# Turning two of the four recurrent-input turns of a hybrid decoder trunk to stationary tokens, with a trip through the scratch in DRAM

## The chip, the cores and the metric

One core of one Trainium2 chip runs the whole kernel. The metric is the device time of one execution in microseconds (us), as the median of repeated runs. The engines are TensorE (PE; its weight loads are PEld), VectorE (DVE), ScalarE (ACT), GpSimd (POOL) and SyncE (SP), whose queue issues nearly all of the DMAs here (SPq in the rows).

## The reference

Two decoder layers on an input of 256 tokens by 2048 channels, all in float32. Layer 0 mixes tokens with a gated recurrent block, layer 1 with causal attention; each is followed by a squared-ReLU MLP of width 8192, and each of the four sub-layers ends in a LayerNorm of `alpha * x + sublayer(x)`. What the change touches is the beginning of layer 0:

```python
gate, u = jnp.split(x @ w_in, 2, axis=-1)          # w_in: 2048 x 4096
u = causal depthwise conv of width 4 over u, + conv_b
r = sigmoid(blockwise u @ gate_a_w + gate_a_b)      # 8 blocks of 256 channels
i = sigmoid(blockwise u @ gate_x_w + gate_x_b)
a = exp(-8 * r * softplus(-lam));  b = u * i * sqrt(1 - a*a)
h = associative scan of h_t = a_t * h_{t-1} + b_t
return (gelu(gate) * h) @ w_out
```

## The kernel before

Every matmul of the large layers is made of three products of rounded parts: each operand is split into a high part and a low remainder (`fp32r`), and high by high, low by high and high by low are added up in PSUM. A weight block is 256 rows (two chunks of 128) by 512 columns. SyncE loads it into one of 4 staging slots (`wst`, `load_block`, L272), ScalarE copies it rounded into one of 8 slots of high parts (`wh`, `split_hi`, L781), VectorE subtracts to get the low part (`wl`, `split_lo`, L1083), and TensorE uses both. The load of block b waits until block b-4 has been split by VectorE (`wl_done`). Eight blocks make a turn: 512 output columns, accumulated over all 2048 rows. The order on every engine is written out by hand: `splits(b, lo, hi)` on ScalarE and on VectorE says which blocks are split between the other pieces of work. `AHEAD` is 7: in turn t these two engines split block 7 and later of the count that starts with the turn's first block, so they work up to 7 blocks ahead of TensorE. `LATE` is 14.

The blocks are numbered through the program. The recurrent input u takes turns 0 to 3 (blocks 0 to 31), the two gate matrices take blocks 32 to 39, the gate branch takes four turns from block 40.

There are two ways to run a turn on TensorE:

- `turn` (L483, L486) keeps a 128 x 128 piece of the weights stationary and moves tokens: for each of 16 chunks and 4 column groups one matmul of 512 columns (high and low tokens side by side, against the high weights) and one of 256 columns (high tokens, low weights). The result has channels on the partitions, and its two halves are in different columns of four banks; ScalarE copies one half out (`take_hl`, L790) and VectorE adds the other (`add_hh`, L1093), which frees the banks (`psum_free`).
- `token_turn` (L495) keeps 128 tokens stationary and moves 512 weight columns: for each chunk six matmuls of 512 columns. The result has tokens on the partitions, in two banks.

Before, all four turns of u use `turn`. The gate branch (blocks 40 to 71) uses `token_turn`; its result must be turned over, since what follows works along the tokens in each channel. ScalarE copies the two banks into a buffer in an order that suits the move (`g_out`, L901) and so frees them; SyncE stores it as four DMAs of 128 KB to a scratch in DRAM (`store_g`, L315) and, once they have landed, loads it back as one DMA of 512 KB with the 32 x 32 squares in place (`read_g`, L321); VectorE transposes within the squares (`turn_g`, L1235, a STREAM_TRANSPOSE). The MLP does the same with its squares (L361, L365, L1453). Both SyncE's waits, for the banks and for the stores, stand in the same queue as the weight loads.

After each turn t of u, the group of four chunks it made goes through the convolution: ScalarE multiplies by the last tap and adds the bias (`conv_start`, L825, four activations), VectorE adds the three other taps (`conv_step`, L1162, four instructions each), ScalarE rounds (`conv_hi_part`, L818), VectorE takes the remainder (`conv_lo`, L1170). Only then can TensorE run the gates of this group. The gates (L588 to L590) are eight pieces `gb`, two for each group, each with 24 matmuls of 256 columns into a pair of banks: gb 0 uses banks 0 and 1, gb 1 banks 2 and 3, gb 2 banks 4 and 5, gb 3 banks 6 and 7, and then again from the start. What TensorE waits for there, ahead of each piece:

```python
            for gb in range(BLOCKS):
                if gb in (0, 2):
                    pe.wait_ge(psum_free, T_G + gb // 2 - 1)
                elif gb >= 4:
                    pe.wait_ge(sig_done, gb - 3)
                pe.wait_ge(pair_ready, R_CONV + 2 * (gb // 2) + 2)
                pe.wait_ge(wl_done, B_GATES + gb + 1)
```

So gb 2 needs the banks of the last turn of u (`psum_free` at 4), and the pieces from gb 4 need the sigmoids of the piece four earlier (`sig_done`, L851, on ScalarE). The softplus of `lambda` is a row of small VectorE instructions (`softplus_start`, L1136 to L1140, `softplus_series`, L1144 to L1150) between the splits.

## Time and profile before

| | |
|---|---|
| Median of 3 runs | 2082.54 us (2081.93 to 2082.73) |
| The profiled execution's own time | 2081.55 us |
| Its span, from the first to the last instruction | 2079.8 us |
| TensorE busy | 2073.0 us, 9438 matmuls |
| VectorE busy | 1267.6 us |
| ScalarE busy | 969.2 us |
| Mean DMA traffic | 217 GB/s |
| Granted TensorE clock in the 40 slices | digit 9 (90% or more of full speed) in each |

The profile is one execution; its own time lies 1.75 us above its span and 0.99 us below the median of the runs. In a timeline row stand the start, the duration, the engine, the line, the operation, output<-inputs, how many instructions are merged, and in brackets the idle time before them with what ended it. Matmuls are pipelined: the row of one is longer than the step from its start to the next start, and it is the step that counts.

### The profile page before, as it was taken

The page shows a single profiled execution, that of the slowest core. Times are in us where ns is not written, and L with a number is a line of the kernel's source. Part 1 is how long each engine was busy: PE and PEld are TensorE (multiplying, and loading weights), DVE is VectorE, ACT ScalarE, POOL GpSimd, SP SyncE. Part 2 cuts the span into 40 slices and gives each one's busy share as a digit, 9 for nine tenths or more (in the row PEclk, how much of TensorE's full clock was granted, in tenths as well). Part 3 has the DMA queues.
Part 4 walks back from the last instruction along what each step waited for, and adds up shares of the span by engine and source line. Part 5 has one row for each costly group of instructions (what it writes and reads, how often), then busy time and mean ns, then how long its engine had stood idle before and what let it go on. Part 6 is the DMA issues. An engine that isn't in the chain of part 4 may idle for free.

```text
span 2079.8 us, 27469 instructions
## 1 busy us (share of the span) xinstructions
PE 2073.0 (100%) x9438; PEld 1724.6 (83%) x9438; DVE 1267.6 (61%) x1247; ACT 969.2 (47%) x1168; POOL 21.3 (1%) x16
## 2 busy tenths in 40 slices
PE   9999999999999999999999999999999999999999
PEld 8888888888888888888888888888888888888887
DVE  6869666665555565555765565775755555555565
ACT  5595555434444443443654444454444434444442
POOL 0000010000000000000100000010000000000000
PEclk9999999999999999999999999999999999999999
DMA  8667758766766766675566667667767766766763
GB/s 259 195 207 243 257 189 264 246 199 206 237 220 185 241 225 200 214 249 173 186 209 206 210 221 233 194 212 243 229 207 221 241 200 201 240 218 224 240 214 120
DMA packets 245884, 451.34 MB, mean 217 GB/s; under 512 B 18720, under 2 KB 49696, under 8 KB 244768
## 3 DMA queue, kind: packets, MB, share of 16 engines
q1 hardware_dynamic: 239888, 440.93, 66.8%
q10 hardware_dynamic: 5904, 9.18, 1.4%
q8 instruction: 58, 0.95, 0.2%
q14 instruction: 34, 0.28, 0.0%
HBM read 421.72 MB, written 20.97 MB: 213 GB/s over the span
## 4 chain that ended last, share of the span: by engine, by line
PE 99%; DMA 0%; DVE 0%; ACT 0%; SPq 0%; issue 0%
PE ps L495 92%; PE ps L486 3%; PE ps L483 1%; PE ps L620 1%; PE ps L589 0%; PE ps L590 0%; PE ps L588 0%; PE ps L658 0%; PE ps L667 0%; DMA f<-in_x_dram 0%; PE ps L668 0%; PE ps L657 0%; PE ps L545 0%; PE ps L681 0%; PE ps L682 0%; DVE f L1335 0%
## 5 line engine op out<-in xcount | busy, mean ns | idle before, releaser
L1083 DVE TENSOR_TENSOR wl<-wst,wh 128x1024 fp32r<-128x1024 f32 x742 | 886.5, 1219 | 380.0 <-ACT wh L781 377.9
L781 ACT ACTIVATE wh<-wst 128x1024 fp32r<-128x1024 f32 x742 | 770.5, 1059 | 690.5 <-PE ps L495 400.6
L495 PE MATMUL ps<-wh,xin 128*128 128x512 f32 x3072 | 824.5, 390 | 0.0
L495 PE MATMUL ps<-wh,hid 128*128 128x512 f32 x2560 | 695.9, 390 | 0.0
L495 PEld LDWEIGHTS ps<-wh,xin 128*128 128x128 f32 x3072 | 575.7, 188 | 118.9
L495 PEld LDWEIGHTS ps<-wh,hid 128*128 128x128 f32 x2560 | 479.5, 188 | 98.9
L495 PE MATMUL ps<-wl,xin 128*128 128x512 f32 x1536 | 472.9, 389 | 0.0
L495 PE MATMUL ps<-wl,hid 128*128 128x512 f32 x1280 | 404.6, 389 | 0.0
L495 PEld LDWEIGHTS ps<-wl,xin 128*128 128x128 f32 x1536 | 288.3, 188 | 60.0
L495 PEld LDWEIGHTS ps<-wl,hid 128*128 128x128 f32 x1280 | 240.2, 188 | 50.0
L1453 DVE STREAM_TRANSPOSE f<-f 128x1024 f32<-128x1024 f32 x32 | 39.9, 1245 | 178.7 <-DMA f<-sq_by_quad 178.7
L975 ACT ACTIVATE hid<-f 128x1024 fp32r<-128x1024 f32 x32 | 34.0, 1063 | 206.5 <-DVE f L1453 206.5
L1280 DVE TENSOR_TENSOR f<-f,ps 128x1024 f32<-128x1024 f32 x36 | 43.9, 1220 | 86.9 <-PE ps L495 86.9
L486 PE MATMUL ps<-xin,wh 128*128 128x512 f32 x256 | 88.8, 397 | 0.0
L1477 DVE TENSOR_TENSOR f<-f 128x1024 f32<-128x1024 f32 x32 | 39.2, 1225 | 74.5 <-ACT f L990 74.3
L990 ACT ACTIVATE f<-ps 128x512 f32<-128x512 f32 x64 | 34.7, 595 | 79.0 <-PE ps L495 79.0
L483 PE MATMUL ps<-xin,wl 128*128 128x256 f32 x256 | 68.5, 278 | 0.0
L486 PEld LDWEIGHTS ps<-xin,wh 128*128 128x128 f32 x256 | 46.9, 188 | 9.5
L483 PEld LDWEIGHTS ps<-xin,wl 128*128 128x128 f32 x256 | 48.1, 188 | 1.4
L1459 DVE TENSOR_TENSOR hid<-f,hid 128x1024 fp32r<-128x1024 f32 x32 | 39.2, 1225 | 3.0
L912 ACT ACTIVATE f<-ps,prm 128x128 f32<-128x128 f32 x96 | 36.2, 480 | 4.1 <-PE ps L620 4.1
L454 POOL TENSOR_SCALAR f<-f,mv,tok 128x512 f32<-128x512 f32 x6 | 19.5, 3259 | 1345.7 <-DVE tok L1310 1345.7
(123 smaller groups left out, 563.8 us busy)
## 6 DMA issues: line engine op xcount, KB each, us to landing
wst<-in_mlp_w_dram SPq DMA_DIRECT2D x512, 512.0 KB, 4.7
wst<-in_moba_w_qkv_dram SPq DMA_DIRECT2D x96, 512.0 KB, 4.6
wst<-in_rg_w_in_dram SPq DMA_DIRECT2D x62, 512.0 KB, 4.5
wst<-in_rg_w_out_dram SPq DMA_DIRECT2D x32, 512.0 KB, 5.6
sq_by_quad<-f SPq DMA_DIRECT2D x128, 128.0 KB, 2.6
f<-sq_by_quad SPq DMA_DIRECT2D x32, 512.0 KB, 4.9
wst<-in_moba_w_out_dram SPq DMA_DIRECT2D x32, 512.0 KB, 5.1
f<-in_x_dram SPq DMA_DIRECT2D x8, 256.0 KB, 6.8
```

Source lines behind the costliest of these rows:

```text
L483: mm = pe.matmul(dst[:, n, 0:T], wl[:, s, w], src[:, c, 0, :], start=False, stop=(c == NC - 1))
L486: pe.matmul(dst[:, n, :], wh[:, s, w], src[:, c, :, :], start=(c == 0), stop=False)
L495: return pe.matmul(dst, src[:, c, part, a * P:(a + 1) * P], (wl if low else wh)[:, s, w], start=(c == 0 and part + low == 0), stop=(c == N ...
L781: act.activation(wh[:, off % SPLITS, :], wst[:, slot, :], ACT.Copy).then_inc(wh_done, 1)
L912: ins = act.activation(norm_t[:, c, h * P:(h + 1) * P], ps[:, bank, q * P:(q + 1) * P], ACT.Identity, scale=prm[:, gain:gain + 1], bias=pr ...
L975: act.activation(hid[:, t * GROUP:(t + 1) * GROUP, 0, :], sq_t, ACT.Copy).then_inc(sq_hi, 1)
L990: act.activation(by_part, by_col, ACT.Relu).then_inc(sq_relu, 1)
L1083: dve.tensor_tensor(wl[:, off % SPLITS, :], wst[:, off % STAGE, :], wh[:, off % SPLITS, :], ALU.subtract).then_inc(wl_done, 1)
L1280: dve.tensor_tensor(res[:, :, cols], res[:, :, cols], banks(half)[:, 0:HALVES, :], ALU.add)\
L1453: dve.transpose(sq_t.rearrange("p c (a i t) -> p i (c a) t", a=HALVES, t=32), quad.rearrange("p i (b r) -> p i b r", r=32)).then_inc(sq_tu ...
L1459: dve.tensor_tensor(hid[:, rows, 1, :], sq_t, hid[:, rows, 0, :], ALU.subtract)\
L1477: dve.tensor_tensor(sqr, sqr, sqr, ALU.mult).then_inc(psum_free, 1)
```

## The change

Turn 1 and turn 2 of u (blocks 8 to 15 and 16 to 23) now run as `token_turn`, in banks 4 and 5 and in banks 0 and 1; turn 0 and turn 3 stay as they are. What the gate branch has for its results, u now shares: the buffers and semaphores are renamed from `g_` to `in_`, the trips are counted through (trips 0 and 1 are u's, 2 to 5 the gate branch's), and ScalarE's copy (`take_in`) frees the banks. `take_hl` and `add_hh` of turns 1 and 2 are gone. VectorE turns the group over (`turn_u`), and `conv_start` of groups 1 and 2 waits for that. The convolution steps of these groups stand later in VectorE's order, and the one of group 2 now stands partly ahead of `add_hh` of turn 3. The order of the loads, the number of weight blocks and the gates' code are unchanged.

```diff
...
+        def turn_of(n):
+            return T_U + 1 + n if n < U_TOKEN else T_G + n - U_TOKEN
...
-            with sp.Fori(1, NG) as t:
-                load_turn(w_in, D + t * COLS, B_U + t * BLOCKS)
-            for gb in range(BLOCKS):
+            def store_in(n):
+                sp.wait_ge(psum_free, turn_of(n) + 1)
+                for i in range(GROUP):
+                    sp.dma_start(to_quad[i], in_out[i * 32:(i + 1) * 32, :, :]).then_inc(in_stored, 16)
+            def read_in(n):
+                sp.wait_ge(in_stored, (n + 1) * (16 * GROUP))
+                if n:
+                    sp.wait_ge(in_turned, n)
+                sp.dma_start(in_quad, by_quad.rearrange("p (i n) -> p i n", i=GROUP)).then_inc(in_back, 16)
+            def move_in(n):
+                return {2: lambda: store_in(n), 3: lambda: read_in(n)}
...
+            def load_gates(gb, b):
                 w, n0 = (rg_gate_a_w, rg_gate_x_w)[gb % 2], gb // 2 * 2
-                sp.wait_ge(wl_done, B_GATES + gb - (STAGE - 1))
+                sp.wait_ge(wl_done, b - (STAGE - 1))
...
+            with sp.Fori(1, NG - 1) as t:
+                load_turn(w_in, D + t * COLS, B_U + t * BLOCKS)
+            load_turn(w_in, D + (NG - 1) * COLS, B_U + (NG - 1) * BLOCKS, move_in(0))
+            also = move_in(1)
+            for gb in range(BLOCKS):
+                if gb in also:
+                    also[gb]()
+                load_gates(gb, B_GATES + gb)
...
-            turn(xin, 1, B_U + BLOCKS, R_X)
-            pair(xin, B_U + 2 * BLOCKS, R_X, T_U + 2)
+            token_turn(xin, 4, B_U + BLOCKS, R_X)
+            pe.wait_ge(psum_free, T_U + 1)
+            token_turn(xin, 0, B_U + 2 * BLOCKS, R_X)
+            pe.wait_ge(psum_free, T_U + 2)
+            turn(xin, 1, B_U + 3 * BLOCKS, R_X)
...
-                act.wait_ge(psum_free, T_U + g + 1)
+                if 1 <= g <= U_TOKEN:
+                    act.wait_ge(in_turned, g)
+                else:
+                    act.wait_ge(psum_free, T_U + g + 1)
...
-            for t in range(NG):
-                b = B_U + t * BLOCKS
-                if t:
-                    splits(b, t, AHEAD, AHEAD + 1)
-                    conv_start(t - 1)
-                    splits(b, t, AHEAD + 1, AHEAD + CONV)
-                    if t == 1:
-                        act.wait_ge(sp_abs, 1)
-                        act.activation(small[:, 1, :], small[:, 0, :], ACT.Exp, scale=-1.0).then_inc(sp_exp, 1)
-                    conv_hi_part(t - 1)
-                splits(b, t, AHEAD + CONV if t else BLOCKS, LATE)
-                take_hl(t % 2, b, u3[:, t * GROUP:(t + 1) * GROUP, :], hl_copied)
-                splits(b, t, LATE)
-            conv_start(NG - 1)
+            def take_in(n, first, b):
+                act.wait_ge(mm_done, b + BLOCKS)
+                if n:
+                    act.wait_ge(in_turned, n)
+                for a in range(HALVES):
+                    by_part = in_out.rearrange("p q (c a r) -> p a c q r", c=GROUP, a=HALVES)[:, a]
+                    by_col = ps[:, first + a, :].rearrange("p (c q r) -> p c q r", c=GROUP, q=GROUP)
+                    taken = act.activation(by_part, by_col, ACT.Copy)
+                taken.then_inc(psum_free, 1)
+            b, no = B_U, 0
+            splits(b, no, BLOCKS, LATE)
+            take_hl(0, b, u3[:, 0:GROUP, :], hl_copied)
+            splits(b, no, LATE)
+            b, no = B_U + BLOCKS, 1
+            splits(b, no, AHEAD, AHEAD + 1)
+            conv_start(0)
+            splits(b, no, AHEAD + 1, AHEAD + CONV)
+            act.wait_ge(sp_abs, 1)
+            act.activation(small[:, 1, :], small[:, 0, :], ACT.Exp, scale=-1.0).then_inc(sp_exp, 1)
+            conv_hi_part(0)
+            splits(b, no, AHEAD + CONV, LATE)
+            take_in(0, 4, b)
+            splits(b, no, LATE)
+            b, no = B_U + 2 * BLOCKS, 2
+            splits(b, no, AHEAD, AHEAD + 6)
+            conv_start(1)
+            splits(b, no, AHEAD + 6, LATE)
+            take_in(1, 0, b)
+            splits(b, no, LATE)
+            b, no = B_U + 3 * BLOCKS, 3
+            splits(b, no, AHEAD, AHEAD + 1)
+            conv_hi_part(1)
+            splits(b, no, AHEAD + 1, AHEAD + 6)
+            conv_start(2)
+            splits(b, no, AHEAD + 6, LATE)
+            take_hl(1, b, u3[:, 3 * GROUP:NC, :], hl_copied)
+            splits(b, no, LATE)
+            conv_hi_part(2)
+            conv_start(3)
...
-            for t in range(NG):
-                b = B_U + t * BLOCKS
-                if t:
-                    splits(b, AHEAD, AHEAD + 1)
-                    for k in range(1, CONV):
-                        splits(b, AHEAD + k, AHEAD + k + 1)
-                        conv_step(t - 1, k)
-                    splits(b, AHEAD + CONV, AHEAD + CONV + 1)
-                    conv_lo(t - 1)
-                    splits(b, AHEAD + CONV + 1, LATE)
-                else:
-                    softplus_abs()
-                    splits(b, BLOCKS, LATE)
-                (lambda: None, softplus_start, softplus_series, lambda: None)[t]()
-                add_hh(t % 2, u3[:, t * GROUP:(t + 1) * GROUP, :], hl_copied, t + 1).then_inc(psum_free, 1)
-                splits(b, LATE)
-            g = NG - 1
-            for k in range(1, CONV):
-                conv_step(g, k)
-            splits(B_GATES, AHEAD, AHEAD + 1)
-            conv_lo(g)
-            splits(B_GATES, AHEAD + 1)
-
-
+            def turn_in(n, dst):
+                dve.wait_ge(in_back, 16 * (n + 1))
+                dve.transpose(dst.rearrange("p c (a i t) -> p i (c a) t", a=HALVES, t=32),
+                              in_quad.rearrange("p i (b r) -> p i b r", r=32)).then_inc(in_turned, 1)
+            def turn_u(g):
+                turn_in(g - 1, u3[:, g * GROUP:(g + 1) * GROUP, :])
...
+            b = B_U
+            softplus_abs()
+            splits(b, BLOCKS, LATE)
+            add_hh(0, u3[:, 0:GROUP, :], hl_copied, 1).then_inc(psum_free, 1)
+            splits(b, LATE)
+            b = B_U + BLOCKS
+            splits(b, AHEAD, AHEAD + 1)
+            for k in range(1, CONV):
+                splits(b, AHEAD + k, AHEAD + k + 1)
+                conv_step(0, k)
+            splits(b, AHEAD + CONV, AHEAD + CONV + 1)
+            conv_lo(0)
+            softplus_start()
+            splits(b, AHEAD + CONV + 1)
+            b = B_U + 2 * BLOCKS
+            splits(b, AHEAD, AHEAD + 2)
+            softplus_series()
+            splits(b, AHEAD + 2, AHEAD + 5)
+            turn_u(1)
+            splits(b, AHEAD + 5, AHEAD + 6)
+            conv_step(1, 1)
+            splits(b, AHEAD + 6, LATE)
+            conv_step(1, 2)
+            splits(b, LATE)
+            conv_step(1, 3)
+            b = B_U + 3 * BLOCKS
+            splits(b, AHEAD, AHEAD + 1)
+            conv_lo(1)
+            splits(b, AHEAD + 1, AHEAD + 5)
+            turn_u(2)
+            splits(b, AHEAD + 5, AHEAD + 6)
+            conv_step(2, 1)
+            splits(b, AHEAD + 6, LATE)
+            conv_step(2, 2)
+            conv_step(2, 3)
+            add_hh(1, u3[:, 3 * GROUP:NC, :], hl_copied, 2).then_inc(psum_free, 1)
+            splits(b, LATE)
+            conv_lo(2)
+            for k in range(1, CONV):
+                conv_step(3, k)
+            splits(B_GATES, AHEAD, AHEAD + 1)
+            conv_lo(3)
+            splits(B_GATES, AHEAD + 1)
```

The first place is SyncE's queue, from the end of the loads of u to the loads of the gate matrices. Before, behind the loop that loads the last turn of u (blocks 24 to 31):

```order
L272 DMA wst<-in_rg_w_in_dram 128x2x512
L304 REGISTER_ALU
L304 COMPARE_AND_BRANCH
L309 DMA wst<-in_rg_gate_a_w_dram 128x4x256 [waits wl_done]
L309 DMA wst<-in_rg_gate_x_w_dram 128x4x256 [waits wl_done]
L309 DMA wst<-in_rg_gate_a_w_dram 128x4x256 [waits wl_done]
```

In the changed kernel (`L277` loads u's blocks 24 and on, `L326` the gate matrices, `L312` stores, `L318` loads back):

```order
L277 DMA wst<-in_rg_w_in_dram 128x2x512 [waits wl_done] x2
L312 DMA sq_by_quad<-spare 32x4x256 [waits psum_free]
L312 DMA sq_by_quad<-spare 32x4x256 x3
L277 DMA wst<-in_rg_w_in_dram 128x2x512 [waits wl_done]
L318 DMA spare<-sq_by_quad 128x1024 [waits in_stored]
L277 DMA wst<-in_rg_w_in_dram 128x2x512 [waits wl_done] x5
L326 DMA wst<-in_rg_gate_a_w_dram 128x4x256 [waits wl_done]
L326 DMA wst<-in_rg_gate_x_w_dram 128x4x256 [waits wl_done]
L312 DMA sq_by_quad<-spare 32x4x256 [waits psum_free]
L312 DMA sq_by_quad<-spare 32x4x256 x3
L326 DMA wst<-in_rg_gate_a_w_dram 128x4x256 [waits wl_done]
L318 DMA spare<-sq_by_quad 128x1024 [waits in_turned,in_stored]
```

Two trips are new: the first stands between the loads of blocks 25 and 27, with block 26 between its parts, the second between those of blocks 33 and 35, with block 34 between. Each load back waits for its stores, and the loads behind it wait with it.

The second place is VectorE while turn 3 of u runs and after it. Before (`L1083` splits a block, `L1093` is `add_hh`, which frees the banks of turn 3):

```order
L1162 SCALAR_TENSOR_TENSOR gate<-f1,prm,gate 128x253 [waits conv_link]
L1162 SCALAR_TENSOR_TENSOR gate<-f1,prm,gate 128x253 x3
L1083 TENSOR_TENSOR wl<-wst,wh 128x1024 [waits mm_done,wh_done]
L1170 TENSOR_TENSOR hid<-gate,hid 128x4x256 [waits conv_hi]
L1083 TENSOR_TENSOR wl<-wst,wh 128x1024 [waits mm_done,wh_done] x2
L1093 TENSOR_TENSOR f1<-f1,ps 128x1024 [waits hl_copied]
L1083 TENSOR_TENSOR wl<-wst,wh 128x1024 [waits mm_done,wh_done]
L1162 SCALAR_TENSOR_TENSOR gate<-f1,prm,gate 128x255 [waits conv_begun]
```

In the changed kernel (`L1117` splits, `L1209` is the transpose of group 2, `L1196` its convolution steps, `L1127` is `add_hh`):

```order
L1117 TENSOR_TENSOR wl<-wst,wh 128x1024 [waits mm_done,wh_done] x4
L1209 STREAM_TRANSPOSE f1<-spare 128x4x8x32 [waits in_back]
L1117 TENSOR_TENSOR wl<-wst,wh 128x1024 [waits mm_done,wh_done]
L1196 SCALAR_TENSOR_TENSOR gate<-f1,prm,gate 128x255 [waits conv_begun]
L1196 SCALAR_TENSOR_TENSOR gate<-f1,prm,gate 128x255 x3
L1117 TENSOR_TENSOR wl<-wst,wh 128x1024 [waits mm_done,wh_done]
L1196 SCALAR_TENSOR_TENSOR gate<-f1,prm,gate 128x254 [waits conv_link]
L1196 SCALAR_TENSOR_TENSOR gate<-f1,prm,gate 128x254 x3
L1196 SCALAR_TENSOR_TENSOR gate<-f1,prm,gate 128x253 [waits conv_link]
L1196 SCALAR_TENSOR_TENSOR gate<-f1,prm,gate 128x253 x3
L1127 TENSOR_TENSOR f1<-f1,ps 128x1024 [waits hl_copied]
L1117 TENSOR_TENSOR wl<-wst,wh 128x1024 [waits mm_done,wh_done]
```

Before, the convolution of group 2 was over when `add_hh` of turn 3 came, with three splits and `conv_lo` between them. Now the transpose and all three of group 2's steps stand ahead of it.

## Rows read from the trace of the kernel before

**Rows 1.** The page: busy time of the engines

```profile
PE 2073.0 (100%) x9438; PEld 1724.6 (83%) x9438; DVE 1267.6 (61%) x1247; ACT 969.2 (47%) x1168; POOL 21.3 (1%) x16
```

**Rows 2.** The chain that ended last: shares, then start, length, what

```profile
PE 99%; DMA 0%; DVE 0%; ACT 0%; SPq 0%; issue 0%
...
122.52 168.67 PE ps L495 x744
```

**Rows 3.** Timeline of TensorE: turn 3, gb 0, gb 2

```profile
77.12 0.63 PE L486 MATMUL ps<-xin,wh 128*128 128x512 f32 x2
...
99.32 0.28 PE L588 MATMUL ps<-hid,wh 128*128 128x256 f32 x1
...
105.07 0.28 PE L588 MATMUL ps<-hid,wh 128*128 128x256 f32 x1
```

**Rows 4.** Timeline of VectorE after block 19

```profile
57.37 1.22 DVE L1170 TENSOR_TENSOR hid<-gate,hid 128x1024 fp32r<-128x1024 f32 x1
...
60.77 0.17 DVE L1136 TENSOR_SCALAR small<-small 128x16 f32<-128x16 f32 x1
...
61.89 1.22 DVE L1093 TENSOR_TENSOR f<-f,ps 128x1024 f32<-128x1024 f32 x1
```

**Rows 5.** Timeline of ScalarE: copy of turn 1, conv_start(3), sigmoids gb 0 to 2

```profile
58.00 1.00 ACT L790 ACTIVATE f<-ps 128x1024 f32<-128x1024 f32 x1
...
103.85 2.08 ACT L825 ACTIVATE gate<-f,prm 128x256 f32<-128x256 f32 x4 [2.08 <-DVE f L1093]
...
108.19 1.57 ACT L851 ACTIVATE f<-ps,prm 128x256 f32<-128x256 f32 x4
...
110.58 1.59 ACT L851 ACTIVATE f<-ps,prm 128x256 f32<-128x256 f32 x4
...
113.91 1.62 ACT L851 ACTIVATE f<-ps,prm 128x256 f32<-128x256 f32 x4
```

**Rows 6.** Timeline of VectorE: add_hh of turn 3, twelve steps of conv 3

```profile
102.60 1.21 DVE L1093 TENSOR_TENSOR f<-f,ps 128x1024 f32<-128x1024 f32 x1
...
105.96 5.06 DVE L1162 SCALAR_TENSOR_TENSOR gate<-f,prm,gate 128x255 f32<-128x255 f32 x12 [1.01 <-ACT gate L825]
```

**Rows 7.** The page: low parts and high parts of the weight blocks

```profile
L1083 DVE TENSOR_TENSOR wl<-wst,wh 128x1024 fp32r<-128x1024 f32 x742 | 886.5, 1219 | 380.0 <-ACT wh L781 377.9
L781 ACT ACTIVATE wh<-wst 128x1024 fp32r<-128x1024 f32 x742 | 770.5, 1059 | 690.5 <-PE ps L495 400.6
```

**Rows 8.** Line L272 (loads of u), 60 to 100 us: time to landing

```profile
DMA to landing us min/median/max: 3.5/4.2/4.7
```

**Rows 9.** Timeline of SyncE: first trip of the gate branch

```profile
147.31 2.63 SPq L315 DMA_DIRECT2D sq_by_quad<-spare  x4
149.98 0.45 SPq L272 DMA_DIRECT2D wst<-in_rg_w_in_dram  x1
153.26 0.34 SPq L321 DMA_DIRECT2D spare<-sq_by_quad  x1
153.65 1.56 SPq L272 DMA_DIRECT2D wst<-in_rg_w_in_dram  x3
```

**Rows 10.** DMAs, 153 to 153.7 us: its load back, and the load behind

```profile
spare<-sq_by_quad SPq DMA_DIRECT2D x1, 512.0 KB, 3.8
wst<-in_rg_w_in_dram SPq DMA_DIRECT2D x1, 512.0 KB, 4.7
```

**Rows 11.** Line L1235, the transposes: ns min/median/max

```profile
L1235 DVE STREAM_TRANSPOSE gate<-spare x4: 1234/1236/1239, 165.4 to 231.8; 128x1024 f32<-128x1024 f32 x4
```

**Rows 12.** Timeline of SyncE: a trip of the MLP

```profile
346.32 1.78 SPq L361 DMA_DIRECT2D sq_by_quad<-f  x4
...
350.37 0.34 SPq L365 DMA_DIRECT2D f<-sq_by_quad  x1
```

**Rows 13.** Timeline of SyncE: third trip of the gate branch

```profile
191.35 1.94 SPq L315 DMA_DIRECT2D sq_by_quad<-spare  x4
...
198.75 0.34 SPq L321 DMA_DIRECT2D spare<-sq_by_quad  x1
```

51 lines of the change are left out of this document (14 added, 37 removed).

## The prediction

> **What bounds the kernel now.** I read the busy times first: TensorE is busy for 2073.0 us of a span of 2079.8 [rows 1]. Then the chain that ended last: 99% of it is TensorE's own work, one matmul behind the other, and 744 of them in the gate branch and after follow each other without a break [rows 2]. So a change can gain only by giving TensorE less to do, and it loses whatever TensorE comes to wait. Last I followed the timelines from 56 to 116 us, to see what is just in time there. The reader is to see one narrow place. TensorE starts piece gb 2 of the gates at 105.07 [rows 3]; it needs the banks that `add_hh` of turn 3 frees, and that ended at 102.60 + 1.21 = 103.81 [rows 6]. The margin is 1.26 us.
>
> **What TensorE saves.** A turn as it was lasts from 77.12 to 99.32, 22.20 us for 128 matmuls [rows 3]. A token turn has 96 matmuls of 512 columns; 168.67 us for 744 of them are 0.2267 us each [rows 2], so 21.76 us. The moved columns are the same, 64 x 768 = 96 x 512 = 49152, 20.48 us at 2.4 GHz; what remains is 1.72 us over 128 and 1.28 us over 96 matmuls, 13.4 ns for each. Two turns save 2 x 0.44 = 0.87 us, all of it on the chain. Bounds: nothing (if what lies around a matmul goes by columns), and 0.87.
>
> The row says 13.4 ns for each matmul beyond its columns. The Trainium skill (TensorE: Matmul & The Clock Gate, "Wait — 56ns, not 53.3ns?") puts that fixed cost at about 2.5 ns, by which 64 matmuls fewer would save only 0.16 us and the sum below would end at 2084.9. The trace disagrees at both matmul sizes, and it decides.
>
> **What moves off VectorE and ScalarE.** `add_hh` of turns 1 and 2 goes (1.22 us each [rows 4]), two transposes of 1.24 us come [rows 11]; ScalarE changes a copy of 1.00 us [rows 5] for a pair of halves of about the same size. Neither engine is the bound (1267.6 and 969.2 us busy [rows 1]). Nothing here is paid for. Turn 1 frees its banks a little earlier than before, turn 3 needs them a whole turn later: nothing.
>
> **What the trips through the scratch make late.** Eight stores of 128 KB and two loads of 512 KB are new, and SyncE's queue holds weight loads behind its wait for the stores. I take a trip at the gate branch's first: 147.31 (first store) to 153.26 (load back), 5.95 us; the next weight load 0.39 later [rows 9]; the load back lands after 3.8, the weight load behind it after 4.7 [rows 10]. It stands in the same traffic, with the same weight loads ahead of it. The ends are 4.05 us (an MLP trip [rows 12]) and 7.40 us [rows 13].
>
> On the trace's clock:
>
> 1. VectorE ends `conv_lo` of group 0 at 58.59. Before, two splits, `softplus_start` (from 60.77, 1.1 us) and `add_hh` (61.89) followed [rows 4]. Now `softplus_start` is first and three splits follow at about 1.14 us from start to start (one alone takes 1.22 [rows 7]): blocks 20, 21 and 22 are ready at 60.8, 62.0 and 63.1. Load 25 goes out at 62.1, the first store at 62.5. ScalarE's copy, in place of the one of 58.00 [rows 5], is long done.
> 2. Load back at 68.4, landed 72.2. The load of block 27 goes out at 68.8 and lands at 73.5. Without the trip it would have gone at about 65.5.
> 3. Block 27's halves take 1.06 and 1.22 us [rows 7]: 75.8. The transpose of group 1 stands behind them: 77.0. `conv_start(1)` takes 2.08 [rows 5]: 79.1. Behind it on ScalarE stands block 29, ready at 79.1 + 1.06 + 1.22 plus overlap and a convolution step, 82.0.
> 4. That releases load 33 (82.1), and then the second trip: stores from 82.5, load back at 88.45, load 35 at 88.9, landed at 93.6 (the common loads land in 3.5 to 4.7 [rows 8]). Its halves are ready at 95.9, and the transpose of group 2 at 97.1.
> 5. `conv_start(2)` to 99.2. A convolution step is a third of 5.06, 1.69 us [rows 6]. The first to 100.9, split 37 to 102.1, the two others to 105.3, `add_hh` of turn 3 to 106.5.
>
> TensorE reaches gb 2 at 105.07 - 0.87 = 104.2. It **waits 2.3 us** for those banks. Nothing gives that back later, since TensorE has no other idle time.
>
> Behind that, `conv_start(3)` waits for the same bank release (as before, 2.08 us idle <- `add_hh` [rows 5]), and the sigmoids follow at their old distances: gb 0 ends at 109.76, 3.83 us after `conv_start(3)`, gb 1 2.41 and gb 2 another 3.36 later [rows 5]. So they end at 112.4, 114.8 and 118.2. TensorE, at 2.88 us a piece, reaches gb 4 at 112.3, gb 5 at 115.2 and gb 6 at 118.1. About 0.2 us more. The last remainder (`conv_lo(3)`) is due for gb 6 too: steps 108.7 to 113.7, rounded by 115.9, ready at 117.2, in time by 0.9.
>
> Elsewhere the weights stay ahead of TensorE: block 27 is ready at 75.8 and used at 84.6, block 35 at 95.9 and used at 107. The cover is 8 us or more; it would go only if a trip took twice its price.
>
> **Sum.** -0.87 + 2.3 + 0.2 = +1.6 us. Against the profiled execution (2081.55) 2083.2; its own time lies 0.99 below the median of the runs, so for the median 2082.54 + 1.6, **2084.2 us**. A measurement of this kernel can tell about 0.2%, 4.2 us, from no change: this forecast is "no change that shows", with the sign slightly bad.
>
> **The rivals.**
>
> *No wait, the saving alone.* If both trips go like the MLP's, 4.05 us, each is 1.9 us shorter and group 2 comes 3.8 us earlier, more than the 2.3 of the wait (load 35 is then bound by the splits, still early enough). Time 2082.54 - 0.87 = 2081.7. For it: the stage of the MLP's trip has the same weight traffic per turn. Against it: the two trips of the gate branch, in the layer that follows at once, took 5.95 and 7.40 [rows 9, 13]. The Trainium skill (DMA: Bandwidth & Descriptors, the fit of fixed and variable cost) gives 2.0 us plus size over 436 GB/s, 2.3 us for a store of 128 KB, which makes a trip even shorter than the MLP's and bears this rival out; the trace's first trips disagree with it.
>
> *Slower: the trips go like the third of the gate branch.* At 7.40 us each adds 1.45, and both stand in one chain (the first delays block 27, that the transpose, that block 29, that the second trip). The wait is 2.5 + 2.9 = 5.4, the time 2082.54 - 0.87 + 5.4 = 2087.1, slower by 0.22%. It decides from the point where the two trips together take 2.5 us more than I priced. For it: that trip has the same sizes, the same queue and nearly the same stage. Against it: the first trip of that stage, with this pattern of loads ahead of it, was the shorter one.
>
> *The saving is not there.* Token turns in this stage could step no faster than the old ones, say because weights stream now where they stood. Then the sum is +2.5, 2085.0. Against it: the same form runs at 0.2267 in all of the later stages.
>
> **How the numbers follow.** The wait of 1 to 4 us: 0.55, and 2084.2 is its middle. No wait to 1 us: 0.25. Slower by more than 0.2% (a wait over 5 us): 0.12. No saving: 0.05. Something that gains elsewhere, by the freed VectorE time at the turn's end: 0.03, most of it too small to show. So faster by over 0.2% 0.02, within 0.2% 0.86, slower 0.12. The range must take in the saving alone with some scatter below it (2081.2) and reach to near the slow trips (2086.8).
>
> **What would show it.** In the changed profile, turns 1 and 2 of u should step at 0.227 us and last 21.76. There should be an idle stretch of TensorE ahead of gb 2 (a matmul of L588's kind), ended by VectorE's `add_hh`; SyncE's waits for the stores, two more of them, near 68 and 88 us; the load of block 35 landing near 94, with ScalarE waiting for it; the transpose of group 2 ending near 97. Wrong would be: no idle time of TensorE before 125 us; an idle stretch ahead of gb 6 or of block 40 in place of gb 2's; or a granted clock that falls behind the wait, which would cost more than the wait itself.

## The result, and the profile after

| | before | after |
|---|---|---|
| Median, both kernels on the same chip | 2082.07 us (2081.47 to 2082.93, 22 runs) | 2085.18 us (2082.43 to 2088.75, 22 runs) |
| Profiled execution's own time | 2081.55 us | 2087.64 us |
| Its span | 2079.8 us | 2085.8 us |
| TensorE busy, matmuls | 2073.0 us, 9438 | 2074.5 us, 9374 |

The changed kernel takes 1.0014 times as long (95% interval 1.0008 to 1.0020): 3.1 us more, within the 0.2% that was called "no change that shows", and within the range given, but nearer to its slow end than to its middle of +1.6. The runs of the changed kernel also scatter over 6 us, where those of before scatter over 1.5. The mean granted clock that each run lists goes with it: six runs at 1.000 took 2082.43 to 2083.56 us, fourteen at 0.999 took 2084.66 to 2087.64, two at 0.998 took 2088.31 and 2088.75. The profiled execution is one of the longer ones (third from the top of the twenty-two); its sum is made against its own time.

The timeline of TensorE in the changed kernel: turn 1 of u, turn 2, turn 3, gb 0, gb 2, a matmul behind it, and the start of the gate branch, to hold against [rows 3]:

```profile
33.18 1.11 PE L507 MATMUL ps<-wh,xin 128*128 128x512 f32 x4
...
55.01 1.07 PE L507 MATMUL ps<-wh,xin 128*128 128x512 f32 x4
...
76.77 0.62 PE L498 MATMUL ps<-xin,wh 128*128 128x512 f32 x2
...
98.96 0.28 PE L596 MATMUL ps<-hid,wh 128*128 128x256 f32 x1
...
109.58 0.39 PE L596 MATMUL ps<-hid,wh 128*128 128x256 f32 x1 [4.71 <-DVE f L1127]
...
111.53 0.41 PE L597 MATMUL ps<-hid,wh 128*128 128x256 f32 x1
...
128.44 0.40 PE L507 MATMUL ps<-wh,xin 128*128 128x512 f32 x1
```

Before, turn 1, turn 2, turn 3, gb 0 and gb 2 started at 32.73, 54.92, 77.12, 99.32 and 105.07, and the gate branch at 122.35. So turns 1 and 2 last 43.59 us in place of 44.39 (-0.80). The gates last 98.96 to 128.44, 29.48 us, in place of 23.03 (+6.45). Turn 1 starts 0.45 later, before anything of the change has run. 0.45 - 0.80 + 6.45 = 6.1, and the two own times differ by 6.09: the whole story lies between 33 and 128 us.

The 6.45 us are two things. From start to start, gb 2 is 4.87 us late (the row's 4.71 counts from the modelled end of the matmul before). The other 1.58 us follow it: the matmuls behind the wait take 0.41 us in their rows instead of 0.28. The windows around the wait in the changed kernel (the granted clock is the third number from the end):

```profile
core 0: us, PE busy (x) PEld busy (x) DVE busy (x) ACT busy (x) POOL busy (x), PEclk, DMA share, GB/s
...
108.00:110.00 2.00, 0.42 (x3) 0.43 (x4) 2.00 (x3) 1.50 (x2) 0.00 (x0) 1.00 0.08 31
110.00:112.00 2.00, 2.00 (x12) 2.00 (x11) 2.00 (x3) 2.00 (x5) 0.00 (x0) 0.50 0.08 15
112.00:114.00 2.00, 2.00 (x13) 2.00 (x13) 1.97 (x6) 1.97 (x3) 0.00 (x0) 0.64 0.73 243
114.00:118.00 4.00, 4.00 (x36) 4.00 (x34) 3.87 (x8) 4.00 (x10) 0.00 (x0) 1.00 0.02 6
```

Behind the wait TensorE runs at 0.50 of its clock, 1.2 GHz, for all of 110 to 112 us and for about 1.4 us of the next two (0.64 on average), some 3.4 us. Of its matmuls, 16 take 0.213 us from start to start in place of 0.120; that is 1.5 us of the 1.58. The rest is 0.10 at the restart.

The chain that ended last in the changed kernel: its shares by engine, and the pieces from 63 to 129 us (start, length, what), to hold against [rows 2]:

```profile
PE 96%; DVE 1%; DMA 1%; issue 1%; ACT 0%; SPq 0%; ACTq 0%; DVEq 0%
...
63.34 4.42 DMA sq_by_quad<-spare
67.77 0.34 SPq L318
68.16 6.19 DMA wst<-in_rg_w_in_dram
74.37 1.07 ACT wh L789
...
76.61 1.25 DVE f L1209
...
89.23 7.44 DMA wst<-in_rg_gate_x_w_dram
96.70 1.07 ACT wh L789
...
98.93 1.25 DVE f L1209
...
108.39 1.14 DVE f L1127
109.58 0.39 PE ps L596
...
128.60 168.68 PE ps L507 x744
```

TensorE no longer carries the chain through here. It runs as the prediction numbered it: the first trip's last store, the load of block 27 behind it, the transpose of group 1 (L1209), the load of block 35, the transpose of group 2, `add_hh` of turn 3 (L1127), gb 2. One piece stands out: load 35 takes 7.44 us to land. From 129 us on nothing differs (168.68 us for the 744 matmuls, before 168.67).

The timeline of SyncE in the changed kernel, both trips:

```profile
61.88 2.02 SPq L312 DMA_DIRECT2D sq_by_quad<-spare  x4
63.94 1.35 SPq L277 DMA_DIRECT2D wst<-in_rg_w_in_dram  x1
67.77 0.34 SPq L318 DMA_DIRECT2D spare<-sq_by_quad  x1
68.16 8.93 SPq L277 DMA_DIRECT2D wst<-in_rg_w_in_dram  x5
...
82.83 0.37 SPq L326 DMA_DIRECT2D wst<-in_rg_gate_x_w_dram  x1
83.24 2.25 SPq L312 DMA_DIRECT2D sq_by_quad<-spare  x4
...
88.85 0.34 SPq L318 DMA_DIRECT2D spare<-sq_by_quad  x1
89.23 1.42 SPq L326 DMA_DIRECT2D wst<-in_rg_gate_x_w_dram  x1
```

First store to load back is 5.89 and 5.61 us, priced 5.95.

The questions for the runs were therefore: is the saving there; which wait makes group 2 late, and is it the second trip as it looks; what would take over if that wait went; and is the clock's fall a matter of the trips or of the wait.

### The profile page after: what moved, and what is told of

It is laid out like the page before. It is cut to its first block, busy times and chain, and to the rows that moved or that the text cites. A ratio compares the mean times of both kernels' runs of the same rounds, so it can differ in the third digit from the quotient of the medians.

```text
span 2085.8 us, 27331 instructions
## 1 busy us (share of the span) xinstructions
PE 2074.5 (99%) x9374; PEld 1724.0 (83%) x9374; DVE 1267.4 (61%) x1247; ACT 969.3 (46%) x1170; POOL 21.3 (1%) x16
## 4 chain that ended last, share of the span: by engine, by line
PE 96%; DVE 1%; DMA 1%; issue 1%; ACT 0%; SPq 0%; ACTq 0%; DVEq 0%
PE ps L507 92%; PE ps L498 1%; DVE gate L1196 1%; PE ps L628 1%; PE ps L495 0%; DMA wst<-in_rg_gate_x_w_dram 0%; PE ps L666 0%; PE ps L675 0%; PE ps L596 0%; PE ps L598 0%; PE ps L597 0%; DMA wst<-in_rg_w_in_dram 0%; PE ps L550 0%; DMA sq_by_quad<-spare 0%; ACT wh L789 0%
## 5 line engine op out<-in xcount | busy, mean ns | idle before, releaser
L1117 DVE TENSOR_TENSOR wl<-wst,wh 128x1024 fp32r<-128x1024 f32 x742 | 886.0, 1219 | 381.3 <-ACT wh L789 379.0
L507 PE MATMUL ps<-wh,xin 128*128 128x512 f32 x3200 | 858.8, 390 | 0.0
L507 PEld LDWEIGHTS ps<-wh,xin 128*128 128x128 f32 x3200 | 599.7, 188 | 123.8
L507 PE MATMUL ps<-wl,xin 128*128 128x512 f32 x1600 | 492.5, 389 | 0.0
L507 PEld LDWEIGHTS ps<-wl,xin 128*128 128x128 f32 x1600 | 300.3, 188 | 62.4
L498 PE MATMUL ps<-xin,wh 128*128 128x512 f32 x128 | 45.2, 401 | 0.0
L495 PE MATMUL ps<-xin,wl 128*128 128x256 f32 x128 | 34.4, 279 | 0.0
L498 PEld LDWEIGHTS ps<-xin,wh 128*128 128x128 f32 x128 | 23.5, 188 | 4.7
L1359 DVE TENSOR_TENSOR f<-f,ps 128x512 f32<-128x512 f32 x8 | 5.5, 687 | 32.1 <-PE ps L507 32.1
```

Source lines behind the costliest of these rows:

```text
L495: mm = pe.matmul(dst[:, n, 0:T], wl[:, s, w], src[:, c, 0, :], start=False, stop=(c == NC - 1))
L498: pe.matmul(dst[:, n, :], wh[:, s, w], src[:, c, :, :], start=(c == 0), stop=False)
L507: return pe.matmul(dst, src[:, c, part, a * P:(a + 1) * P], (wl if low else wh)[:, s, w], start=(c == 0 and part + low == 0), stop=(c == N ...
L1117: dve.tensor_tensor(wl[:, off % SPLITS, :], wst[:, off % STAGE, :], wh[:, off % SPLITS, :], ALU.subtract).then_inc(wl_done, 1)
```

## The experiments

Each was run beside the kernel before on the same chip, eleven runs each unless said. Ratios are to the kernel before, with 95% intervals. "Late" is from start to start, as above, in the profiled execution. That is one of the eleven and need not be a typical one.

### The saving alone

The trips of u are left out: VectorE turns the buffer over where it lies. Groups 1 and 2 of u therefore hold wrong numbers; all else is computed as before.

```diff
-            load_turn(w_in, D + (NG - 1) * COLS, B_U + (NG - 1) * BLOCKS, move_in(0))
-            also = move_in(1)
+            load_turn(w_in, D + (NG - 1) * COLS, B_U + (NG - 1) * BLOCKS)
+            also = {}
```

> The changed kernel with u's two trips through the scratch left out: VectorE transposes ScalarE's copy of turns 1 and 2 where it lies, without the 32 x 32 squares having been moved, so groups 1 and 2 of u hold wrong numbers. TensorE's work, the splits, the copies and the transposes stay. Theory (the saving is 0.87 us and all the loss comes from the two trips): no idle time of TensorE at the gates, turns 1 and 2 of u 21.76 us each, 0.9 us under the kernel before, about 2081.2. Rival (token turns save nothing here): as the kernel before, 2082.1. Rival (the order of VectorE's work makes the wait, not the trips): the wait ahead of gb 2 stays, 2084 to 2085.

Measured: 2080.81 us (2080.33 to 2081.00), before 2081.91 (2081.45 to 2083.11, 29 runs); ratio 0.9993 (0.9985 to 1.0002). The interval takes in 1, but the slowest of the runs is below the fastest of before. The timeline of TensorE in this kernel, turn 2, turn 3 and gb 0:

```profile
54.66 1.07 PE L507 MATMUL ps<-wh,xin 128*128 128x512 f32 x4
...
76.42 0.62 PE L498 MATMUL ps<-xin,wh 128*128 128x512 f32 x2
...
98.61 0.28 PE L596 MATMUL ps<-hid,wh 128*128 128x256 f32 x1
```

The token turn lasts 21.76 us, as priced, and the gates 23.03, as before. The saving is real: from turn 1 to the gate branch this execution takes 0.85 us less, the medians differ by 1.1.

### Which of the two waits in SyncE's queue

First the second trip's load back was moved behind the loads of blocks 35 and 36, so that load 35 doesn't wait for the stores.

```diff
-            also = move_in(1)
+            also = {2: lambda: store_in(1), 5: lambda: read_in(1)}
```

> The changed kernel with the second trip's load back placed behind the loads of blocks 35 and 36 instead of ahead of 35; the first trip as it is. Theory (SyncE's queue holds load 35 behind the wait for the stores, and block 35 holds the transpose of group 2): load 35 goes out at about 87 to 89 and lands some 3 us earlier than the 96.67 of the changed profile, the transpose ends near 97 and not 100.2, the wait ahead of gb 2 falls from 4.7 to about 2, and the median from 2085.2 to about 2083.5; the clock falls in fewer runs. Rival (the bytes in flight are the limit, not the order of the queue): load back and loads 35 to 38 end as late as before, 2085.2.

Measured: 2084.89 us (2082.29 to 2087.28), before 2081.91; ratio 1.0015 (1.0006 to 1.0024). In the profiled execution (2083.04 us, the second fastest of the eleven) load 35 went out at 87.26 and landed 4.1 us later, the load back went out at 90.16 and landed at 95.70, and gb 2 was 2.0 us late. So this took away the long landing, but put the load back in its place: the transpose of group 2 came at 95.72. The wait of 2.0 us is what was expected, but the median missed the expected 2083.5 by 1.4: it is only 0.3 us below the changed kernel's, and the clock fell in eight of the eleven runs, going by their times and mean clocks. The second wait alone isn't the answer.

Then turn 2 was given back its old form, so that only the first trip is left (the order of group 2's work on ScalarE and VectorE goes back with it).

```diff
-U_TOKEN = 2
+U_TOKEN = 1
...
-            token_turn(xin, 0, B_U + 2 * BLOCKS, R_X)
+            turn(xin, 0, B_U + 2 * BLOCKS, R_X)
```

> Only turn 1 of u is a token turn with its trip; turn 2 is as in the kernel before, with its copy and sum, and VectorE's order for groups 2 and 3 is that of before. Theory (one token turn saves 0.44 us, the first trip has a whole turn to spare, and only the second is late): no idle time of TensorE at the gates, the clock stays, 2081.9 - 0.44 = 2081.5, with the narrow scatter of the kernel before. Rival (each trip costs, the first by holding the loads of blocks 27 to 29): a wait ahead of gb 2 or in turn 3, 2083 or more.

Measured: 2084.70 us (2083.30 to 2086.00), before 2081.95; ratio 1.0014 (1.0005 to 1.0023). The expectation was missed by 3 us. The profiled execution is the fastest of the eleven, at 2083.30. The timeline of TensorE and that of ScalarE in this kernel, gb 2 and `conv_start(2)`:

```profile
106.61 0.39 PE L596 MATMUL ps<-hid,wh 128*128 128x256 f32 x1 [1.74 <-DVE f L1127]
```

```profile
87.44 2.07 ACT L836 ACTIVATE gate<-f,prm 128x256 f32<-128x256 f32 x4
```

Before, `conv_start(2)` was at 84.69. The one trip, which belongs to group 1, makes group 2 2.75 us late too, the margin was 1.26 [rows 3, 6], and gb 2 comes 1.9 us late. This was the first sign that the first trip does the harm.

Last the trips were taken off SyncE's queue, one, the other or both. GpSimd, which has nothing to do in this stretch, issues them (`by_pool` is the number of the trip; with both, it is a loop over them):

```diff
+            n = by_pool
+            pool.wait_ge(psum_free, turn_of(n) + 1)
+            for i in range(GROUP):
+                pool.dma_start(to_quad[i], in_out[i * 32:(i + 1) * 32, :, :]).then_inc(u_stored, 16)
+            pool.wait_ge(u_stored, 16 * GROUP)
+            if n:
+                pool.wait_ge(in_turned, n)
+            pool.dma_start(in_quad, by_quad.rearrange("p (i n) -> p i n", i=GROUP)).then_inc(u_back, 16)
```

Both by GpSimd, and the same again in a later batch:

> The changed kernel with u's two trips (eight stores, two loads back) issued and waited for by GpSimd, so SyncE's queue holds nothing behind them. Theory (the loads held in the queue are half of the delay): loads 27 and 35 go out when the blocks four earlier are split, 3 us and 1 to 2 us earlier, and the transpose of group 2 comes 2 to 4 us earlier than in the changed kernel; the wait ahead of gb 2 falls to 0 to 1 us and the median to 2081.5 to 2083. Rival (the trip's own length sets it, and GpSimd's is longer, since it writes its descriptors itself): the load back comes later than by SyncE, the wait grows, 2086 or more.

> The kernel with GpSimd's trips once more, unchanged, to see whether its place under the kernel before holds: 2080.9 to 2081.7 against 2081.9, no idle time of TensorE over 0.5 us, the narrow scatter of before. If the first result was luck: a part of the runs above 2083, as the changed kernel has them.

Measured: 2081.28 us (2080.67 to 2081.87), before 2081.95, ratio 0.9997 (0.9988 to 1.0006); and 2081.09 us (2080.55 to 2081.44), before 2081.79 (2081.42 to 2082.60, 21 runs), ratio 0.9996 (0.9987 to 1.0005). The timeline of GpSimd in the first of the two:

```profile
59.54 2.39 POOL L467 DMA_DIRECT2D sq_by_quad<-spare  x4 [56.95 <-ACT spare L860]
66.76 0.57 POOL L471 DMA_DIRECT2D spare<-sq_by_quad  x1 [4.83 <-DMA sq_by_quad<-spare]
80.57 2.19 POOL L467 DMA_DIRECT2D sq_by_quad<-spare  x4 [13.25 <-ACT spare L860]
86.94 0.56 POOL L471 DMA_DIRECT2D spare<-sq_by_quad  x1 [4.19 <-DMA sq_by_quad<-spare]
```

The trips are slower here (first store to load back 7.2 and 6.4 us), but nothing stands behind them. gb 2 is 0.3 us late in the one and not late in the other; the gates last 23.57 and 23.03 us.

The first by GpSimd, the second by SyncE as in the changed kernel:

> The changed kernel with the first trip issued by GpSimd and the second by SyncE. Theory (the delays of the two trips add up in one chain, and each is the hold of the weight loads behind it): about half of what GpSimd's two trips win back, a wait of 0.5 to 1.5 us ahead of gb 2, 2082 to 2083, the clock mostly unhurt. Rival (only the second trip counts, since there is a turn of time after the first): as the changed kernel, 2085.

Measured: 2081.22 us (2080.66 to 2085.05; ten of the eleven up to 2082.22), before 2081.63; ratio 0.9999 (0.9990 to 1.0008). gb 2 is 0.3 us late. The second trip's wait in SyncE's queue costs nothing that shows in the time.

The first by SyncE, the second by GpSimd, and the same again:

> The changed kernel with the first trip issued by SyncE and the second by GpSimd. Theory (as for its twin): about half as well, 2082 to 2083.5. Rival (only the second counts): 2081.2, as with both trips by GpSimd. Rival (only the first counts, as the run with one token turn hints, which had no second trip and still waited 1.9 us): 2084.5 or more.

> The kernel of m2_second_by_pool once more, to see whether the long landing of load 35 (7.7 us there, 4.5 us in e4_pool, which issued it at the same time) belongs to the kernel or to that one execution. If it belongs to the kernel: load 35 lands after 7.0 to 8.0 us again, TensorE waits 2.5 to 4 us at gb 2, and the median is 2084.5 to 2086. If it was chance of one execution: load 35 lands after 4 to 5.5 us, TensorE waits under 1 us at gb 2, and the profiled run is near 2082, whatever the median. The first is likelier, since eight of eleven runs of m2_second_by_pool were above 2084.

Measured: 2085.42 us (2082.83 to 2087.95), before 2081.63, ratio 1.0017 (1.0008 to 1.0026); and 2084.70 us (2082.70 to 2086.80), before 2081.99, ratio 1.0012 (1.0003 to 1.0021). gb 2 was 3.0 and 3.1 us late. That is the changed kernel again, with the second trip away from SyncE.

What differs inside. Issue and landing of a load are read from the profiled execution of each, in us; the transpose and `add_hh` are given by their starts:

| trips: first, second | block 27 landed | transpose of group 1 starts | load 33 out | load 35 out | it lands after | `add_hh` starts | gb 2 late |
|---|---|---|---|---|---|---|---|
| SyncE, SyncE (changed) | 74.35 | 76.61 | 82.83 | 89.23 | 7.4 | 108.31 | 4.9 |
| SyncE, GpSimd | 72.74 | 75.00 | 81.22 | 86.64 | 7.7 | 105.99 | 3.0 |
| the same again | 74.22 | 76.48 | 82.70 | 88.12 | 6.7 | 106.45 | 3.1 |
| GpSimd, SyncE | 70.47 | 73.77 | 80.00 | 86.16 | 5.5 | 103.25 | 0.3 |
| GpSimd, GpSimd | 71.03 | 75.01 | 81.23 | 86.66 | 4.5 | 103.91 | 0.3 |
| the same again | 70.33 | 73.61 | 79.83 | 85.25 | 4.5 | 102.30 | 0 |

With the first trip in SyncE's queue block 27 goes out at 68.1 to 68.4 and lands at 72.7 to 74.4; without it, out at 63.4 to 64.5 and landed by 71.0. By load 33 the difference is between nothing (81.22 against 81.23) and 3.0 us. And load 35 takes 1.2 to 3.2 us longer to land in all three executions with that trip by SyncE. The DMA views of two kernels for this load alone, SyncE then GpSimd, and both by GpSimd; it was issued at 86.64 and 86.66:

```profile
wst<-in_rg_gate_x_w_dram SPq DMA_DIRECT2D x1, 512.0 KB, 7.7
```

```profile
wst<-in_rg_gate_x_w_dram SPq DMA_DIRECT2D x1, 512.0 KB, 4.5
```

What goes out next is the same in these two (GpSimd's load back at 86.86 and 86.94, the next weights at 89.07 and 89.08). The repeat said that the long landing belongs to the kernel (6.7 us, a little under the 7 to 8 expected). What in the first trip causes it 20 us later, the runs don't show. The trace shows where in the load it sits: each load counts up its semaphore in sixteen parts. With both trips by GpSimd fifteen parts of load 35 are in after 3.92 and 4.24 us and the last after 4.5. With SyncE then GpSimd fourteen are in after 3.94 us, just as early, and the last two after 5.41 and 7.71; in the repeat thirteen after 3.87, the last after 6.70. In the changed kernel fifteen are in after 5.57 and the last after 7.44. So one to three late parts make the long landing. A first trip by SyncE isn't enough for it: with the load back of the second trip moved behind, or with no second trip, load 35 landed after 4.1 and 3.9 us.

Between the first executions of "SyncE, GpSimd" and of "GpSimd, GpSimd" that landing is the whole difference: load 35 goes out at the same time and lands 3.16 us later, the transpose of group 2 starts 3.16 later (96.61 against 93.45), and `add_hh` 2.08, since with both trips by GpSimd ScalarE still waits for load 36.

Against "GpSimd, SyncE", the changed kernel's `add_hh` is 5.06 us later: 3.07 of it load 35 going out later, 1.99 its longer landing. So the runs show that a first trip by SyncE makes the loss, and that it does so in two ways: the loads held behind it, by up to 3 us, and the long landing, whose cause stays open.

### Order in the engines' queues

`add_hh` of turn 3 ahead of the last two convolution steps of group 2, which frees the banks earlier but makes group 2 later:

```diff
+            add_hh(1, u3[:, 3 * GROUP:NC, :], hl_copied, 2).then_inc(psum_free, 1)
             conv_step(2, 2)
             conv_step(2, 3)
-            add_hh(1, u3[:, 3 * GROUP:NC, :], hl_copied, 2).then_inc(psum_free, 1)
```

> The changed kernel with add_hh of turn 3 ahead of the second and third convolution step of group 2 on VectorE, not behind them. Theory (the banks and the first sigmoid are due at about the same time, since conv_start(3) also stands behind the rounding of group 2 on ScalarE): the wait at gb 2 falls by 3.4 us, to about 1.3 as in the profiled run, and one of 3 to 5 us comes ahead of gb 4, for the sigmoids of gb 0; the median stays or rises by up to 1.2, 2085 to 2086.5. Rival (the banks alone make the wait): 3 us come off, about 2082.

Measured: 2086.88 us (2084.18 to 2088.33), before 2081.91, ratio 1.0022 (1.0014 to 1.0031); one more run took 6691.47 us at full clock and is left out of the range as disturbed. The timeline of TensorE in this kernel, its one idle stretch in the gates:

```profile
113.81 0.58 PE L596 MATMUL ps<-hid,wh 128*128 128x256 f32 x1 [3.46 <-ACT f L892]
```

The wait at gb 2 is gone and one of 3.6 us stands at gb 4, on the sigmoids of gb 0, as expected (the median is 0.4 us above the expected range): ScalarE had `conv_start(3)` in front of them, and that stands behind the rounding of group 2. The banks were only the nearer of two waits.

With both trips by GpSimd, the split of block 36 behind the start of convolution 2 on ScalarE, and on VectorE (not shown here) behind the first step of that convolution:

```diff
-            splits(b, no, AHEAD + 1, AHEAD + 6)
+            splits(b, no, AHEAD + 1, AHEAD + 5)
             conv_start(2)
-            splits(b, no, AHEAD + 6, LATE)
+            splits(b, no, AHEAD + 5, LATE)
```

> The kernel with GpSimd's trips, and block 36 moved behind the start of group 2's convolution: on ScalarE conv_start(2) ahead of the high part of block 36, on VectorE the first convolution step of group 2 ahead of its low part. In the run before it ScalarE waited for load 36 (landed 94.83) with the transposed group 2 ready at 94.69. Theory (the rest of the wait, 0.26 us ahead of gb 2 and 0.28 at the sigmoids, is the same chain a little late): conv_start(2) about 1 us earlier, no wait at all, 0.3 to 0.5 us less, about 2080.9, the value without trips (2080.8). Rival (another thing is due then, the split of block 36 or 37): no change, 2081.3.

Measured: 2081.46 us (2080.48 to 2081.86), before 2081.79; ratio 0.9998 (0.9989 to 1.0007); gb 2 0.6 us late. No gain over the same kernel in the old order; the expectation was missed.

### The clock's fall without any trip

The kernel before, with three or with five sums of 128 x 1024 added on VectorE in turn 3 of u, whose results nobody reads:

```diff
                 (lambda: None, softplus_start, softplus_series, lambda: None)[t]()
+                if t == 3:
+                    for k in range(5):
+                        idle = spare[:, k % 2 * 1024:(k % 2 + 1) * 1024]
+                        link(dve.tensor_tensor(idle, f1[:, 0:1024], f1[:, 0:1024], ALU.add))
```

> The kernel before with three sums in place of five ahead of add_hh of turn 3: 3 x 1.26 = 3.8 us of work, margin 1.26, by the five-sum run's measure (4.5 waited where 5.0 was worked out) a wait of 2.0 to 2.5 us, and up to 0.3 for the sigmoids. If a wait of this length never brings the granted clock down: about 2084.3 in all runs. If it does in some: a part of the runs 1 to 2 us longer at a mean clock of 0.999, the scatter of the changed kernel. If always: about 2086.

> The kernel before, with five sums of 128 x 1024 on VectorE (into a buffer not used then) ahead of add_hh of turn 3; nothing else. They take 5 x 1.26 = 6.3 us, the margin was 1.26, so TensorE waits 5.0 us ahead of gb 2, and 0.2 more for the sigmoids. Theory (after a wait of this length the granted clock falls to half for a while, as the changed profile has it: 0.50 and 0.64 in the two stretches behind the wait, 1.6 us lost): 2082.1 + 5.2 + 1.6 = 2088.9, and the clock row falls in every run. Rival (a wait costs its own length, and the clock fall of the changed kernel has another cause, such as its DMAs): 2087.3.

Measured with three: 2084.58 us (2084.05 to 2087.58), before 2081.95, ratio 1.0016 (1.0007 to 1.0025); gb 2 2.5 us late, no fall of the clock in the profiled execution. Eight runs at a mean clock of 1.000 took up to 2085.72 us, three at 0.999 took 2086.15 to 2087.58. With five, five runs: 2089.71 us (2088.26 to 2090.54), before 2081.91, ratio 1.0036 (1.0023 to 1.0049); gb 2 4.5 us late. The windows of the kernel with five, columns as above:

```profile
106.00:108.00 2.00, 0.00 (x0) 0.00 (x0) 1.93 (x3) 0.00 (x0) 0.00 (x0) 1.00 0.29 111
108.00:110.00 2.00, 0.00 (x0) 0.00 (x0) 1.97 (x2) 0.00 (x0) 0.00 (x0) 0.91 0.00 0
...
112.00:114.00 2.00, 2.00 (x11) 2.00 (x11) 1.67 (x4) 1.98 (x3) 0.00 (x0) 0.50 0.66 187
...
116.00:118.00 2.00, 2.00 (x17) 2.00 (x17) 2.00 (x5) 2.00 (x5) 0.00 (x0) 0.88 0.00 0
```

The clock falls before TensorE has started again (0.91 in 108 to 110, where no matmul runs; the restart is at 110.23) and stays at 0.50 to beyond 116 us, 6.8 us in all; the gates last 30.34 = 23.03 + 4.49 + 2.82, so what follows the wait costs more than the 1.8 expected. No transfer of turns 1 and 2 to or from the scratch takes part, so it is the wait that brings the fall, whoever causes it.

## Why the prediction came out as it did

**The sign, the place and the order of the chain were right.** The numbered steps, forecast and measured in the changed kernel:

| step | forecast | measured |
|---|---|---|
| 1: first store; 2: load 27 out, landed | 62.5; 68.8, 73.5 | 61.88; 68.16, 74.35 |
| 3: transpose of group 1 ends | 77.0 | 77.85 |
| 4: second trip's first store | 82.5 | 83.24 |
| 4: load 35 out, landed | 88.9, 93.6 | 89.23, 96.67 |
| 4: transpose of group 2 ends | 97.1 | 100.17 |
| 5: `add_hh` of turn 3 ends | 106.5 | 109.53 |
| wait at gb 2 | 2.3 | 4.87 |
| behind the wait | 0.2 | 1.58 |
| saving of two turns | -0.87 | -0.80 (-0.85 without trips) |

**The saving held.** 13.4 ns for each matmul beyond its columns gave 21.76 us a turn. Turn 2 takes 21.76 in the changed kernel and without trips, turn 1 21.83 and 21.79. The Trainium skill (TensorE: Matmul & The Clock Gate, "Wait — 56ns, not 53.3ns?") has 2.5 ns, by which the two turns would save an estimated 0.16 us; the measured 0.80 to 0.85 speaks against it for these fp32r matmuls.

**But in the changed kernel it bought nothing.** `add_hh` sets the start of gb 2 there, at 109.58 whatever TensorE did before: 109.58 - 105.07 = 4.51 us late, and with the 1.58 behind it that is the whole +6.1. TensorE's saving only made its wait longer. The prediction's sums for a smaller saving overlook this: with banks due at 106.5 and no saving, TensorE would wait 1.4 us in place of 2.3, and the sum stays at +1.6. The +2.5 (2085.0) of the rival without a saving, and the 2084.9 worked out for a saving of 0.16, are wrong.

**The mis-sized term is load 35 in step 4.** Up to its issue the chain was 0.3 us behind the forecast. The load was priced at 4.7 us to landing, from "the common loads land in 3.5 to 4.7 [rows 8]"; it took 7.44. The steps behind it kept their lengths (the transpose ends 3.5 us after the landing in both columns, `add_hh` 9.4 after that), so `add_hh` is 3.0 us later than forecast; TensorE itself arrives 0.5 later, most of it the late start of turn 1, and 2.6 us of miss in the wait remain. The price was taken from a stretch in which loads go out singly, and used for one in which they go out in a bunch behind a held queue. That is a part of the miss: in the changed kernel the five loads of L277 from 63.9 to 72.4 us already land after 5.8 to 7.0 us:

```profile
DMA to landing us min/median/max: 5.8/6.2/7.0
```

Fifteen of the sixteen parts of load 35 are in after 5.57 us, which fits that. The last part, 1.9 us behind them, bunching doesn't explain: with SyncE then GpSimd load 35 goes out 2.7 us behind one load and 2.4 ahead of the next, as with both by GpSimd, and still takes 7.7.

**The two trips were priced alike, and they are not alike.** Both were given 5.95 us in one chain, and step 4 let the second hold load 35 from 82.5 to 88.9. The first alone in SyncE's queue gives 2084.7 to 2085.4 us; the second alone gives 2081.22. Why the second costs so little can be read from the queue. From load 33 to load 35 it is 6.2 and 6.4 us with the second trip in the queue and 5.4 without, in each of the four: that load had to wait for the splits of block 31 nearly as long anyway, and the trip adds 0.7 to 1.0.

**Behind the wait: the sigmoids were sized right, the clock was left out.** The executions in which the clock stayed up (three sums, one token turn, the load back moved, SyncE then GpSimd again) have 0.27 to 0.29 us in their gates beyond the wait: 0.10 at the restart and 0.17 to 0.19 at gb 4, the "about 0.2 us more" of the sigmoids. The fall of the clock was named as what would make the forecast wrong, and had no term and no chance in the sum. It cost 1.5 us in the profiled execution, 1.3 net, since no wait for the sigmoids is left behind it. In the twenty-two runs, those at 1.000 take 0.4 to 1.5 us more than the median of before, which is the forecast of +1.6 or under it; the other sixteen, 2.6 or more, make the median. The wait of 4.9 us and the clock together took the profiled execution to +6.1, well beyond the range, so that the range held the median and not every run. A part of the median's closeness is luck: in the twenty-two runs the kernel before is at 2082.07 and not 2082.54, so the difference was missed by 1.5 us (+3.1 for +1.6) and the time, 2085.18 for 2084.2, by only 1.0.

**The rivals.** "No wait, the saving alone" (2081.7, 0.25) has the time of the kernels whose first trip is issued by GpSimd, 2081.1 to 2081.3, but not for its reason: it asked for shorter trips, and GpSimd's are longer (6.3 to 7.2 us from the first store to the load back). What counts is what stands behind them. SyncE's eight stores in the changed kernel landed after 3.6 to 4.4 us, not after the 2.3 worked out beside this rival. "The trips go like the third of the gate branch" is out: they took 5.89 and 5.61. "The saving is not there" is out.

**Open.** Why the last parts of load 35 come late where the first trip was SyncE's and the second trip's load back goes out beside it; and what decides between a fall of the clock and none at nearly the same wait.

**A version without the loss.** Both trips by GpSimd: 2081.28 and 2081.09 us against 2081.95 and 2081.79 for the kernel before, 0.7 us or 0.03% less. The intervals of the ratio take in 1, so that it is ahead of the kernel before isn't shown by them; in the second set nine of the eleven runs lie below the fastest of the 21 of before, and the other two within 0.02 us of it. If the 0.7 us are real, they are most of the saving of 0.87. It is 4 us ahead of the changed kernel.

## What to carry to other kernels

A wait in a queue that also issues the weight loads is paid by what stands behind it, so read the queue's followers before the transfer's own length, and put such a trip on an engine with nothing else to issue. Price a load by the landing times of loads that go out as closely bunched as it will, not by the common ones, and leave room for one late part, which alone made 1.9 us here. A saving ahead of a wait is lost in the wait: take it off once. Where TensorE comes to wait, even for the 2 to 3 us of these kernels, give the clock's fall a term and a chance of its own: here a wait of 3.0 us was followed by 1.6 us more and one of 3.1 us, in the same kernel, by 0.3; behind waits of 3.6 to 4.9 us it was 1.6 to 2.8.

## What the runs showed of the hardware that was not expected

The granted clock of TensorE fell to 0.50, 1.2 GHz, behind waits of 3.0 us (SyncE then GpSimd), 3.6 (`add_hh` early), 4.5 (five sums) and 4.9 (the changed kernel); it did not behind 1.9, 2.0 and 2.5 us, nor behind 3.1 in the repeat of the first of these. It stayed there for 3.4 us in the first and the last of these, and for 6.8 us in the other two. With five sums it fell while TensorE stood idle, 0.6 us before the restart; in the changed kernel 0.4 us after it, and with SyncE then GpSimd 0.8 us after it. The same kernel differs from run to run: with five sums all five runs list a mean clock below 1.000, in the changed kernel sixteen of twenty-two, with three sums three of eleven. Such a mean alone is no proof for one run, since three runs with both trips by GpSimd list 0.999 at 2081.12 to 2081.87 us. The clock also falls at the very end of the program, where it costs nothing: in the profile of the kernel before the stretch 2078.0 to 2079.7 us, with no matmul in it, has 0.64.

GpSimd's queue moved the same bytes as SyncE's: with both trips by GpSimd four stores of 128 KB were issued in 2.4 and 2.2 us (in the changed kernel SyncE took 2.0 and 2.3), and its load back of 512 KB landed after 5.5 and 5.6 us (SyncE's after 5.2 and 3.7).

A load of 512 KB, issued at the same moment with the same neighbours, landed after 4.5 us in one kernel and 7.7 (6.7 in the repeat) in another that differed only in which queue had carried a transfer some 20 us earlier. Fourteen of its sixteen parts were in after 3.9 us in both; a load's landing is that of its last part.
